# Hybrid decoder step on one core: key pass with eight page slots, weight pairs on ScalarE's queue, paired transposes and narrower stationary queries

## The chip, the cores and the metric

The kernel runs on one core of a Trainium2 chip. The metric is the device time of one execution in microseconds (us). TensorE is called PE below, its weight loads PEld, VectorE DVE, ScalarE ACT, GpSimd POOL, SyncE SP.

## The reference

One inference step of a two-layer decoder. The prompt has 512 tokens, and beside it 8 sequences decode 4 new tokens each; the width is 2048. All data are float32.

1. Layer 0: `[b, c, h, z] = rmsnorm(x) W_in`, `y = (silu(z) * b * conv3(c * h)) W_out`, `x = x + y`.
2. Keys and values, shared by all later layers: `k, v = rmsnorm(x) W_kv`; k is normalised per head (16 half heads of 128) and its first 32 components are rotated.
3. Layer 1, differential attention: `q, z = rmsnorm(x) W_in_b`; q is normalised and rotated like k. Prompt queries attend causally to prompt keys; each of the 8 sequences attends to 2048 past keys, which lie in 16 pages of 128 keys in a paged cache (`cache_k`, `cache_v`, `page_table`), and to its 4 new keys. `w = softmax(s0) - lambda * softmax(s1)`, `o = w v`, `y = (rmsnorm(o) * silu(z)) W_out_b`.

What the changed code computes is the projections of point 2 and 3, and the past scores of the 8 sequences:

```python
k_past = cache_k[page_table].reshape(n_seq, past, N_HEADS, 2, HEAD_DIM)
s_past = jnp.einsum('bqhcd,bkhcd->bhcqk', q, k_past, preferred_element_type=jnp.float32)
```

## The kernel before

The program runs six stages one after the other: `read_inputs`, `conv_in`, `conv_out`, `project_and_score`, `attention`, `project_out`. Only `project_and_score` (line 677 on) changes.

**Projections.** The stage makes 64 blocks of 128 output columns, called steps n = 0 to 63: 16 of q, 16 of z, 16 of k, 16 of v. A weight block is split into a high and a low part, and PE multiplies x_hi and x_lo by w_hi (line 1032, 64 matmuls of 272 columns) and then x_hi by w_lo (line 1040, 32 matmuls). Weights come as pairs of blocks of 2 MB each (`load_pair`, line 778, issued on SP's queue) into two buffers. ACT scales a pair by the norm gain in 16 instructions (`scale_pair`, line 834), makes w_hi (`split_hi`, line 848), and DVE makes w_lo (`split_lo`, line 947). DVE takes the result of a block out of PSUM (`evacuate`, lines 956 and 958), and after a squared sum (PE line 1048) and ACT's rsqrt it finishes the tile (`finish`, lines 971 to 986). ACT stores the tile to a scratch in HBM (`store`, line 854) three steps later; tiles of k and v are also turned on PE (lines 1062, 1065), copied (lines 859, 860) and written out (lines 862, 864).

**Key pass.** Beside steps 18 to 63 the stage computes the past scores. The keys of one sequence and one half of the heads are 16 half pages of 512 KB; there are 256 of them. SP loads them (`load_keys`, line 790) into a ring of six slots. The work is cut into 128 units; four half pages make two units, an even and an odd one. DVE transposes a unit in blocks of 32x32 with four instructions (`turn_unit`, line 996) into one of two buffers; PE then multiplies it (`score`, line 1081): 16 float32 matmuls of 128 columns, which the profile shows as 32, since each is run as two. The stationary operand is 32 columns wide, of which 16 can be other than zero: 4 queries in each of 4 blocks of rows, laid in `q_blocks` by ACT (`lay_queries`, line 890). The four column groups of the array work side by side. A slot is free when both units of its pages have been transposed.

**Order.** Each engine's instructions are one list in program order. How many units a step gets is written in `UNITS_IN_STEP`. Unit A stands before `finish` on DVE and in the middle of the step on PE, C at the end, and D after it:

```python
for n in range(N):                      # DVE
    evacuate(n - 1)
    turn_unit(units["A"])
    finish(n - 2)
    split_lo(n + 1)
    for at in "BCD": turn_unit(units[at])
```

(shortened: units that a step lacks are left out.) On PE a step is: first half of line 1032, D of the step before, second half, A, squared sum of n - 1, first half of line 1040, B, `turn_tile(n - 2)`, second half, C. On ACT a step is: `square(n - 1)`, `split_hi(n + 1)`, `store(n - 3)`, `norm_scale(n - 1)`, in some steps `lay_queries` and `move_scores`, and in even steps `scale_pair(n // 2 + 1)`. SP's list has `load_pair(n // 2 + 1)` at the start of every even step and four `load_keys` for each odd unit. `finish` and, for v, `evacuate` write into one of two tiles, and wait until the store of the tile two steps earlier has landed (`scratch_out`).

Of the kernel before, what the change touches and what calls it, by code (L numbers as in the profile page):

```python
# [21 lines left out]
ALU = mybir.AluOpType  # L22
# [616 lines left out]
NRING = 6  # L639
# [7 lines left out]
UNITS_IN_STEP = [2, 2, 2, 3] * 4 + [3, 3, 3, 2] * 4 + [4, 3, 4, 3, 3, 4, 3] * 2  # L647
# [31 lines left out]
def project_and_score(nc, m, d, st):  # L679
# [10 lines left out]
    with ExitStack() as ctx:  # L690
# [8 lines left out]
        swap = sb("swap", [ROT, T])  # L699
        cos, sin = sb("cos", [ROT, T]), sb("sin", [ROT, T])  # L700
        rows = [sb(f"rows{s}", [P, TT * P]) for s in range(2)]
        srows = [sb(f"srows{s}", [GS, G * P]) for s in range(2)]
        pages = sb("page_ids", [1, NSEQ * NPG], I32)
        ring = [sb(f"ring{s}", [P, HALF]) for s in range(NRING)]
        kth = [sb(f"keys_turned{f}", [P, GRP * QUAD]) for f in range(2)]
        qblk = [sb(f"q_blocks{f}", [P, HALF]) for f in range(2)]
# [10 lines left out]
        rows_out = [sem(f"rows_out{s}") for s in range(2)]  # L717
        page_in = [sem(f"page_in{s}") for s in range(NRING)]
        blank, qblk_ready, kt_ready, unit_scored = sem("blank"), sem("qblk_ready"), sem("kt_ready"), sem("unit_scored")
# [27 lines left out]
        def rows_in_slot(n):  # L747
            return sum(turns(x) for x in range(n % 2, n, 2))

# [16 lines left out]
        def _(sp):  # L766
# [3 lines left out]
            def load_pair(p):  # L770
                w, col0, _ = head_weights(d, KINDS[2 * p // KT])
                col = col0 + (2 * p % KT) * P
                if p == 1:
                    sp.wait_ge(lo_ready, 1)
                else:
                    sp.wait_ge(block_done, 2 * p - 2)
                sp.sem_inc(granted, 1)
                sp.dma_start(tiles(m.PAIR_RAW[p % 2]),
                             w.rearrange("(k p) n -> p k n", p=P)[:, :, col:col + 2 * P]).then_inc(pair_in[p % 2], 16)

            def load_keys(n):
# [8 lines left out]
                sp.dma_start(ring[n % NRING][:, :], cache_k[ds(page, 1), :, hh * HALF:(hh + 1) * HALF]  # L790
# [29 lines left out]
        def _(act):  # L820
# [4 lines left out]
            scratch = {"q": d["q_scratch"], "k": d["k_scratch"], "z": d["z_scratch"]}  # L825

# [23 lines left out]
            def store(n):  # L850
# [5 lines left out]
                if turns(n):  # L856
                    act.wait_ge(turned, turns_before(n) + 1)
                    after(act, rows_out[s], rows_in_slot(n) * 32)
                    act.activation(rows[s][:, :], m.PS[:, ROWS, :], ACT.Copy).then_inc(rows_ready, 1)
                    act.activation(srows[s][:, :], m.PS[0:GS, SROWS, 0:G * P], ACT.Copy).then_inc(rows_ready, 1)  # L860
                    act.wait_ge(rows_ready, turns_before(n) * 2 + 2)
                    act.dma_start(out_p[kind][:, :, local * P:(local + 1) * P],
                                  rows[s][:, :].rearrange("p (t c) -> p t c", t=TT)).then_inc(rows_out[s], 16)
                    act.dma_start(out_s[kind][:, :, local * P:(local + 1) * P],
                                  srows[s][:, :].rearrange("p (g c) -> p g c", g=G)).then_inc(rows_out[s], 16)
# [17 lines left out]
            def lay_queries(half):  # L883
# [4 lines left out]
                for b in range(P // TURN):  # L888
                    for c in range(4):
                        ins = act.activation(  # L890
                            qblk[half % 2][b * TURN:(b + 1) * TURN, :].rearrange("p (m c x) -> p m c x", m=PART, c=4)
# [43 lines left out]
            for s in range(2):  # L935
                act.wait_ge(scratch_out[s], 16 * kept_in_slot(N + s))
                act.wait_ge(rows_out[s], 32 * rows_in_slot(N + s))
# [89 lines left out]
        def _(pe):  # L1027
# [40 lines left out]
            def score(u):  # L1068

                half, b = u // 8, u // 4  # L1070
                if u % 8 == 0:
                    pe.wait_ge(qblk_ready, half + 1)
# [738 lines left out]
```

## Time and profile before

| | |
|---|---|
| time, median of 3 runs | 2752.18 us (2747.29 to 2761.38) |
| the profiled execution: its time, its span | 2754.07 us, 2752.3 us |
| granted TensorE clock, mean | 0.956 of full speed |
| busy share of the span: PE, PEld, DVE, ACT, POOL | 90%, 81%, 54%, 37%, 13% |
| `project_and_score` | 1033.0 to 2073.2 us of the span |
| of it, steps 18 to 63 with the key pass | 1273.6 to 2057.3 us |

A line of the profile names the line of the kernel, the engine and the operation, what is written and what is read (out<-in, buffer numbers left out) and its shape. In a timeline a row gives the start and the length in us, xcount if several equal instructions are merged, and in square brackets the idle time of that engine just before, with what ended it. A DMA's row is only its issue; how long it took to land is told in a line of its own.

### The profile page before, as it was taken

To read this page: it belongs to the slowest core of one execution; us is meant where nothing else is said; L and a number is where in the kernel's file an instruction comes from. 1 tells how busy PE (TensorE), PEld (TensorE's weight loads), DVE (VectorE), ACT (ScalarE), POOL (GpSimd) and SP (SyncE) were. 2 spreads that over 40 slices of the span, in tenths; PEclk is the share of its full clock that TensorE was granted. 3 is DMA by queue.
4 is the path that set the end of the run, shared out by engine and by line. 5 is a ranking of instruction groups with operands and counts; after the bars stand their busy time and mean duration, and the time that the engine had idled before them with its cause. 6 is when DMAs were issued, how large, how long until landed. Compare 5 with 4: busy or idle time off the path is not lost. (4 is left out here: it accounts for less than half of the span.)

```text
span 2752.3 us, 52718 instructions
## 1 busy us (share of the span) xinstructions
PE 2481.1 (90%) x21599; PEld 2229.3 (81%) x21599; DVE 1494.2 (54%) x1926; ACT 1017.1 (37%) x1826; POOL 346.9 (13%) x142
## 2 busy tenths in 40 slices
PE   6999999999999999999999999989995556656998
PEld 5999999999999989999898999978882122213998
DVE  3565565666563343456888887766664334324221
ACT  4121111112112226776445687745541212224121
POOL 5233333233320110000000000000000110010000
PEclk9999999999999999999999999999997778877999
DMA  4323332323323323244766778778869989986343
GB/s 129 92 77 92 92 92 76 92 83 85 92 76 112 112 86 99 85 153 135 248 237 239 268 266 267 266 243 267 281 231 361 385 343 374 381 363 245 113 120 87
DMA packets 387584, 512.01 MB, mean 186 GB/s; under 512 B 12618, under 2 KB 319700, under 8 KB 370964
## 3 DMA queue, kind: packets, MB, share of 16 engines
q1 hardware_dynamic: 328436, 449.67, 48.1%
q10 hardware_dynamic: 57792, 55.74, 5.8%
q0 software_dynamic: 1200, 4.46, 0.4%
q8 instruction: 106, 1.74, 0.3%
q14 instruction: 50, 0.41, 0.0%
HBM read 470.87 MB, written 38.94 MB: 185 GB/s over the span
## 5 line engine op out<-in xcount | busy, mean ns | idle before, releaser
L1032 PE MATMUL psum<-x_hi,w_hi 128*128 128x272 f32 x2048 | 434.2, 293 | 3.0 <-PEq L503 3.0
L106 PE MATMUL psum<-x_hi,w_hi 128*128 128x272 f32 x2048 | 427.0, 289 | 8.4 <-DVEq L413 8.4
L106 PE MATMUL psum<-x_lo,w_hi 128*128 128x272 f32 x2048 | 426.2, 289 | 0.0
L1032 PE MATMUL psum<-x_lo,w_hi 128*128 128x272 f32 x2048 | 426.0, 289 | 0.0
L996 DVE STREAM_TRANSPOSE h_keys_turned<-h_ring 128x512 f32<-128x512 f32 x512 | 325.1, 682 | 144.3 <-DMA h_ring<-in_cache_k_dram 140.6
L1032 PEld LDWEIGHTS psum<-x_hi,w_hi 128*128 128x128 f32 x2048 | 321.7, 190 | 18.8 <-issue 18.8
L106 PEld LDWEIGHTS psum<-x_hi,w_hi 128*128 128x128 f32 x2048 | 321.5, 189 | 9.5 <-ACTq L405 9.1
L1032 PEld LDWEIGHTS psum<-x_lo,w_hi 128*128 128x128 f32 x2048 | 322.4, 189 | 0.0
L106 PEld LDWEIGHTS psum<-x_lo,w_hi 128*128 128x128 f32 x2048 | 320.9, 188 | 0.0
L366 POOL TENSOR_TENSOR w_raw<-w_raw,params 128x2048 f32<-128x2048 f32 x63 | 245.9, 3903 | 509.6 <-DMA w_raw<-in_w_in_a_dram 502.7
L1040 PE MATMUL psum<-x_hi,w_lo 128*128 128x272 f32 x2048 | 287.1, 296 | 0.0
L1040 PEld LDWEIGHTS psum<-x_hi,w_lo 128*128 128x128 f32 x2048 | 267.0, 190 | 9.4 <-issue 5.9
L114 PE MATMUL psum<-x_hi,w_lo 128*128 128x272 f32 x2048 | 266.4, 287 | 0.0
L114 PEld LDWEIGHTS psum<-x_hi,w_lo 128*128 128x128 f32 x2048 | 260.2, 188 | 0.0
L834 ACT ACTIVATE w_raw<-w_raw,params 128x256 f32<-128x256 f32 x496 | 201.6, 495 | 103.9 <-DMA w_raw<-in_w_kv_dram 58.6
L385 ACT ACTIVATE w_hi<-w_raw 128x2048 fp32r<-128x2048 f32 x64 | 122.4, 1912 | 305.1 <-PE psum L114 280.4
L422 DVE TENSOR_TENSOR w_lo<-w_raw,w_hi 128x2048 fp32r<-128x2048 f32 x64 | 175.5, 2742 | 104.1 <-ACT w_hi L385 104.1
L947 DVE TENSOR_TENSOR w_lo<-w_raw,w_hi 128x2048 fp32r<-128x2048 f32 x63 | 143.6, 2280 | 54.6 <-ACT w_hi L848 54.6
L1081 PE MATMUL psum<-h_keys_turned,h_q_blocks 128*32 128x128 f32 x4096 | 141.2, 280 | 35.1 <-DVE h_keys_turned L996 34.9
L1489 PE MATMUL psum<-head 128*128 128x128 f32 (+3 forms) x128 | 49.3, 518 | 126.4 <-DMA head<-out_new_v_prompt_dram 125.7
L1533 PE MATMUL psum<-ring,weights 128*8 128x512 f32 x1024 | 146.0, 671 | 8.0 <-DMA ring<-in_cache_v_dram 8.0
L1081 PEld LDWEIGHTS psum<-h_keys_turned,h_q_blocks 128*32 128x32 f32 x4096 | 106.4, 111 | 55.8 <-DVE h_keys_turned L996 29.3
(207 smaller groups left out, 3134.7 us busy)
## 6 DMA issues: line engine op xcount, KB each, us to landing
h_ring<-in_cache_k_dram SPq DMA_DIRECT2D x256, 512.0 KB, 6.1
ring<-in_cache_v_dram SPq DMA_DIRECT2D x128, 1024.0 KB, 12.5
w_raw<-in_w_in_a_dram SPq DMA_DIRECT2D x64, 1024.0 KB, 6.2
w_raw<-in_w_kv_dram SPq DMA_DIRECT2D x16, 2048.0 KB, 12.7
w_raw<-in_w_in_b_dram SPq DMA_DIRECT2D x15, 2048.0 KB, 9.6
w_raw<-in_w_out_a_dram SPq DMA_DIRECT2D x16, 1024.0 KB, 5.6
f_raw<-in_w_out_b_dram SPq DMA_DIRECT2D x16, 1024.0 KB, 6.1
x_scratch<-x ACTq DMA_DIRECT2D x16, 272.0 KB, 2.0
```

The source lines that it names most:

```text
L106: pe.matmul(out[:, g, 0:GT], m.WH[s][:, k * P:(k + 1) * P], x[:, k * T + g * GT:k * T + (g + 1) * GT], start=(k == 0 and x is xh), stop=Fa ...
L114: last = pe.matmul(out[:, g, 0:GT], m.WL[s][:, k * P:(k + 1) * P], xh[:, k * T + g * GT:k * T + (g + 1) * GT], start=False, stop=(k == KT ...
L366: pool.tensor_tensor(tiles(raw[p % 2][:, :]), tiles(raw[p % 2][:, :]), m.PAR[:, GA:GA + KT].unsqueeze(2).to_broadcast([P, KT, P]), ALU.mul ...
L385: act.activation(m.WH[p % 2][:, :], raw[p % 2][:, :], ACT.Copy).then_inc(hi_ready, 1)
L422: dve.tensor_tensor(m.WL[p % 2][:, :], raw[p % 2][:, :], m.WH[p % 2][:, :].bitcast(F32), ALU.subtract).then_inc(lo_ready, 1)
L834: ins = act.activation(wk, wk, ACT.Copy, scale=m.PAR[:, gain + k:gain + k + 1])
L947: dve.tensor_tensor(columns(m.PAIR_LO, n), src, tiles(m.WH[n % 2][:, :].bitcast(F32)), ALU.subtract).then_inc(lo_ready, 1)
L996: dve.transpose(kth[u % 2][:, s * QUAD:(s + 1) * QUAD], ring[n % NRING][:, u % 2 * QUAD:(u % 2 + 1) * QUAD]).then_inc(kt_ready, 1)
L1032: pe.matmul(psum[n % 2][:, g, 0:GT], m.WH[n % 2][:, k * P:(k + 1) * P], x[:, k * T + g * GT:k * T + (g + 1) * GT], start=(k == 0 and x is ...
L1040: last = pe.matmul(psum[n % 2][:, g, 0:GT], w[:, k, :], m.XH[:, k * T + g * GT:k * T + (g + 1) * GT], start=False, stop=(k == KT - 1), ski ...
L1081: last = pe.matmul(bank[a * TURN:(a + 1) * TURN, u // 2 % 2, :, u % 2, :], qblk[half % 2][:, ch * TURN:(ch + 1) * TURN], keys[:, :, a * 4 ...
L1533: last = pe.matmul(out[c * B:c * B + 2 * NEW, :], wt[r % 2][:, weights_at(p, c):weights_at(p, c) + 2 * NEW], ring[(r * NPG + p) % NR][:, c ...
```

## The change

1. The ring of half pages has eight slots in place of six, as one buffer, and a `turn_unit` is two instructions of 128x1024 elements (two pages each) in place of four of 128x512.
2. `load_pair` moves from SP to ACT: at step 0 after `split_hi(1)`, and in even steps after `split_hi(n + 1)`, before `store(n - 3)`.
3. `q_blocks` has 16 columns per block in place of 32, so the score matmul has a stationary operand of 16 columns and writes 16 of each 32 rows of PSUM; DVE sets the two banks to zero once at the start.
4. `rows` and `srows`, the buffers from which k and v tiles are written out, become single; `swap` lies in `r`.
5. `UNITS_IN_STEP` is spread otherwise: 2 or 3 units in the steps of z, three in nearly all of v.

```diff
-NRING = 6
+NRING = 8
+QN = P // 32 * NEW
-UNITS_IN_STEP = [2, 2, 2, 3] * 4 + [3, 3, 3, 2] * 4 + [4, 3, 4, 3, 3, 4, 3] * 2
+UNITS_IN_STEP = [2, 3] * 8 + [3, 3, 3, 2] * 4 + [3, 3, 4, 3, 3, 3, 3] * 2
...
-        rows = [sb(f"rows{s}", [P, TT * P]) for s in range(2)]
-        srows = [sb(f"srows{s}", [GS, G * P]) for s in range(2)]
+        rows = sb("rows", [P, TT * P])
+        srows = sb("srows", [GS, G * P])
-        ring = [sb(f"ring{s}", [P, HALF]) for s in range(NRING)]
+        ring = sb("ring", [P, NRING * HALF])
-        qblk = [sb(f"q_blocks{f}", [P, HALF]) for f in range(2)]
+        qblk = [sb(f"q_blocks{f}", [P, HALF // TURN * QN]) for f in range(2)]
...
         def _(sp):
-            def load_pair(p):
-                w, col0, _ = head_weights(d, KINDS[2 * p // KT])
-                col = col0 + (2 * p % KT) * P
-                if p == 1:
-                    sp.wait_ge(lo_ready, 1)
-                else:
-                    sp.wait_ge(block_done, 2 * p - 2)
-                sp.sem_inc(granted, 1)
-                sp.dma_start(tiles(m.PAIR_RAW[p % 2]),
-                             w.rearrange("(k p) n -> p k n", p=P)[:, :, col:col + 2 * P]).then_inc(pair_in[p % 2], 16)
...
-                    sp.wait_ge(kt_ready, (2 * (before // GRP) + 1) * GRP + before % GRP + 1)
+                    sp.wait_ge(kt_ready, (2 * (before // GRP) + 1) * 2 + before % GRP // 2 + 1)
...
-            load_pair(1)
             sp.wait_ge(ids_in, 16)
             for n in range(N):
-                if n % 2 == 0 and n and n + 2 < N:
-                    load_pair(n // 2 + 1)
...
         def _(act):
+            def load_pair(p):
+
+                w, col0, _ = head_weights(d, KINDS[2 * p // KT])
+                col = col0 + (2 * p % KT) * P
+                if p == 1:
+                    act.wait_ge(lo_ready, 1)
+                else:
+                    act.wait_ge(block_done, 2 * p - 2)
+                act.dma_start(tiles(m.PAIR_RAW[p % 2]), w.rearrange("(k p) n -> p k n", p=P)[:, :, col:col + 2 * P]).then_inc(pair_in[p % 2], 16)
...
                 if turns(n):
                     act.wait_ge(turned, turns_before(n) + 1)
-                    after(act, rows_out[s], rows_in_slot(n) * 32)
+                    after(act, rows_out, turns_before(n) * 32)
...
             scale_second()
+            split_hi(1)
+            load_pair(1)
...
-                if n + 1 < N:
+                if n and n + 1 < N:
                     split_hi(n + 1)
+                if n and n % 2 == 0 and n + 2 < N:
+                    load_pair(n // 2 + 1)
                 if n >= 3:
                     store(n - 3)
...
             def turn_unit(u):
 
                 after(dve, unit_scored, u - 1)
-                for s in range(GRP):
-                    n = u // 2 * GRP + s
+                for pair in range(GRP // 2):
+                    n = u // 2 * GRP + 2 * pair
                     if u % 2 == 0:
-                        dve.wait_ge(page_in[n % NRING], 16 * (n // NRING + 1))
-                    dve.transpose(kth[u % 2][:, s * QUAD:(s + 1) * QUAD],
-                                  ring[n % NRING][:, u % 2 * QUAD:(u % 2 + 1) * QUAD]).then_inc(kt_ready, 1)
+                        for x in (n, n + 1):
+                            dve.wait_ge(page_in[x % NRING], 16 * (x // NRING + 1))
+                    dve.transpose(kth[u % 2][:, pair * 2 * QUAD:(pair + 1) * 2 * QUAD].rearrange("p (s x) -> p s x", s=2),
+                                  ring[:, n % NRING * HALF:(n % NRING + 2) * HALF].rearrange("p (s x) -> p s x", s=2)
+                                  [:, :, u % 2 * QUAD:(u % 2 + 1) * QUAD]).then_inc(kt_ready, 1)
...
+            dve.memset(m.PS[:, KEYS[0]:KEYS[0] + 2, :], 0.0).then_inc(blank_banks, 1)
...
-                pe.wait_ge(kt_ready, (u + 1) * GRP)
+                pe.wait_ge(kt_ready, (u + 1) * 2)
...
-                        last = pe.matmul(bank[a * TURN:(a + 1) * TURN, u // 2 % 2, :, u % 2, :],
-                                         qblk[half % 2][:, ch * TURN:(ch + 1) * TURN], keys[:, :, a * 4 + c, :],
+                        last = pe.matmul(bank[a * TURN:a * TURN + QN, u // 2 % 2, :, u % 2, :],
+                                         qblk[half % 2][:, ch * QN:(ch + 1) * QN], keys[:, :, a * 4 + c, :],
```

## Rows read from the trace of the kernel before

**Rows 1.** Windows: stretch, PE, PEld, DVE, ACT, POOL busy, PE clock, DMA share, GB/s.

```profile
1273.60:1495.30 221.70, 209.74 (x2339) 197.82 (x2337) 188.80 (x217) 107.99 (x253) 0.00 (x0) 0.98 0.67 230
1495.30:1765.10 269.80, 267.84 (x3060) 249.76 (x3056) 221.52 (x323) 200.70 (x406) 0.00 (x0) 1.00 0.79 264
1765.10:1784.40 19.30, 17.36 (x208) 16.04 (x203) 14.18 (x22) 11.88 (x24) 0.00 (x0) 1.00 0.88 311
1784.40:1808.90 24.50, 17.73 (x202) 16.25 (x198) 13.28 (x21) 15.19 (x39) 0.00 (x0) 0.93 0.41 134
1808.90:1828.50 19.60, 16.40 (x203) 15.23 (x199) 12.11 (x17) 5.67 (x16) 0.00 (x0) 1.00 0.95 333
1828.50:2057.30 228.80, 219.51 (x2706) 203.38 (x2702) 152.06 (x215) 114.86 (x299) 0.00 (x0) 0.99 0.80 267
```

**Rows 2.** Waits, 1273.6 to 2057.3: total us, times, longest.

```profile
DVE h_keys_turned L996 <- DMA h_ring<-in_cache_k_dram: 140.6, 85, 5.0
...
PE psum L1081 <- DVE h_keys_turned L996: 34.9, 23, 5.4
...
DVE h_tile L956 <- DMA k_scratch<-h_tile: 12.8, 2, 9.9
```

**Rows 3.** Timeline of PE and PEld around a score unit, and one step later.

```profile
1701.57 1.08 PE L1081 MATMUL psum<-h_keys_turned,h_q_blocks 128*32 128x128 f32 x32
1702.58 0.30 PEld L1032 LDWEIGHTS psum<-x_hi,w_hi 128*128 128x128 f32 x2 [0.20 <-issue]
...
1718.82 1.08 PE L1081 MATMUL psum<-h_keys_turned,h_q_blocks 128*32 128x128 f32 x32
```

**Rows 4.** Timeline of PE, cut 0.03 and 0.18 us into this unit.

```profile
1701.57 0.32 PE L1081 MATMUL psum<-h_keys_turned,h_q_blocks 128*32 128x128 f32 x4
...
1701.57 0.43 PE L1081 MATMUL psum<-h_keys_turned,h_q_blocks 128*32 128x128 f32 x8
```

**Rows 5.** Value matmuls of `attention`: timeline of PEld, and the stretch's window row.

```profile
2092.58 0.15 PEld L1533 LDWEIGHTS psum<-ring,weights 128*8 128x8 f32 x4 [0.70 <-issue]
...
2090.90:2095.20 4.30, 4.29 (x24) 0.73 (x24) 1.90 (x2) 0.00 (x0) 0.00 (x0) 0.50 1.01 419
```

**Rows 6.** Timeline of DVE, one unit transposed.

```profile
1352.41 2.47 DVE L996 STREAM_TRANSPOSE h_keys_turned<-h_ring 128x512 f32<-128x512 f32 x4
```

**Rows 7.** Landing of line 778 (pairs, from 1273.6), 790 (pages), 854 (scratch), in this order.

```profile
DMA to landing us min/median/max: 9.3/12.4/14.1
...
DMA to landing us min/median/max: 3.1/6.1/11.3
...
DMA to landing us min/median/max: 2.4/6.7/11.0
```

**Rows 8.** Timeline of steps 26 and 27 (z): a pair is scaled, split, and unit C follows.

```profile
1413.00 6.51 ACT L834 ACTIVATE w_raw<-w_raw,params 128x256 f32<-128x256 f32 x16 [6.84 <-DMA w_raw<-in_w_in_b_dram]
...
1419.96 1.90 ACT L848 ACTIVATE w_hi<-w_raw 128x2048 fp32r<-128x2048 f32 x1
...
1423.81 2.29 DVE L947 TENSOR_TENSOR w_lo<-w_raw,w_hi 128x2048 fp32r<-128x2048 f32 x1
...
1428.54 1.08 PE L1081 MATMUL psum<-h_keys_turned,h_q_blocks 128*32 128x128 f32 x32 [0.45 <-DVE h_keys_turned L996]
```

**Rows 9.** Timeline of step 49, the second of v.

```profile
1791.52 0.53 ACTq L854 DMA_DIRECT2D k_scratch<-h_tile  x1
...
1796.09 0.72 DVE L956 TENSOR_TENSOR h_tile<-psum,rs 128x544 f32<-128x544 f32 x1 [9.88 <-DMA k_scratch<-h_tile]
...
1799.26 1.94 PE L1081 MATMUL psum<-h_keys_turned,h_q_blocks 128*32 128x128 f32 x32 [5.36 <-DVE h_keys_turned L996]
```

**Rows 10.** Timeline of the stage's end: the last two tiles written out.

```profile
2066.64 0.38 ACTq L862 DMA_DIRECT2D out_new_v_prompt_dram<-h_rows  x1
...
2068.30 0.60 ACT L859 ACTIVATE h_rows<-psum 128x512 f32<-128x512 f32 x1 [1.69 <-PE psum L1065]
```

**Rows 11.** Timeline of the stage's start.

```profile
1034.86 4.79 ACT L841 ACTIVATE w_raw<-w_raw,params 128x128 f32<-128x128 f32 x16 [2.14 <-POOL h_q_blocks L817]
```

More of the change, by code:

```diff
@@ L716, in project_and_score @@
         scratch_out = [sem(f"scratch_out{s}") for s in range(2)]
-        rows_out = [sem(f"rows_out{s}") for s in range(2)]
+        rows_out = sem("rows_out")
         page_in = [sem(f"page_in{s}") for s in range(NRING)]
+        blank_banks = sem("blank_banks")
         blank, qblk_ready, kt_ready, unit_scored = sem("blank"), sem("qblk_ready"), sem("kt_ready"), sem("unit_scored")
@@ L745, in kept_in_slot @@
             return sum(kind_of(x) != "v" for x in range(n % 2, n, 2))
-        def rows_in_slot(n):
-            return sum(turns(x) for x in range(n % 2, n, 2))
         def after(eng, sem_, n):
@@ L786, in load_keys @@
                     before = n - NRING
-                    sp.wait_ge(kt_ready, (2 * (before // GRP) + 1) * GRP + before % GRP + 1)
+                    sp.wait_ge(kt_ready, (2 * (before // GRP) + 1) * 2 + before % GRP // 2 + 1)
                 page = sp.value_load(pages[0:1, i * NPG + p:i * NPG + p + 1], min_val=0, max_val=n_phys - 1)
                 sp.sem_inc(granted, 1)
-                sp.dma_start(ring[n % NRING][:, :], cache_k[ds(page, 1), :, hh * HALF:(hh + 1) * HALF]
+                sp.dma_start(ring[:, n % NRING * HALF:(n % NRING + 1) * HALF], cache_k[ds(page, 1), :, hh * HALF:(hh + 1) * HALF]
                              .rearrange("o p n -> (o p) n")).then_inc(page_in[n % NRING], 16)
@@ L857, in store @@
                     act.wait_ge(turned, turns_before(n) + 1)
-                    after(act, rows_out[s], rows_in_slot(n) * 32)
-                    act.activation(rows[s][:, :], m.PS[:, ROWS, :], ACT.Copy).then_inc(rows_ready, 1)
-                    act.activation(srows[s][:, :], m.PS[0:GS, SROWS, 0:G * P], ACT.Copy).then_inc(rows_ready, 1)
+                    after(act, rows_out, turns_before(n) * 32)
+                    act.activation(rows[:, :], m.PS[:, ROWS, :], ACT.Copy).then_inc(rows_ready, 1)
+                    act.activation(srows[:, :], m.PS[0:GS, SROWS, 0:G * P], ACT.Copy).then_inc(rows_ready, 1)
                     act.wait_ge(rows_ready, turns_before(n) * 2 + 2)
                     act.dma_start(out_p[kind][:, :, local * P:(local + 1) * P],
-                                  rows[s][:, :].rearrange("p (t c) -> p t c", t=TT)).then_inc(rows_out[s], 16)
+                                  rows[:, :].rearrange("p (t c) -> p t c", t=TT)).then_inc(rows_out, 16)
                     act.dma_start(out_s[kind][:, :, local * P:(local + 1) * P],
-                                  srows[s][:, :].rearrange("p (g c) -> p g c", g=G)).then_inc(rows_out[s], 16)
+                                  srows[:, :].rearrange("p (g c) -> p g c", g=G)).then_inc(rows_out, 16)
             def square(n):
@@ L890, in lay_queries @@
                         ins = act.activation(
-                            qblk[half % 2][b * TURN:(b + 1) * TURN, :].rearrange("p (m c x) -> p m c x", m=PART, c=4)
+                            qblk[half % 2][b * TURN:(b + 1) * TURN, :].rearrange("p (m c x) -> p m c x", m=PART, c=4, x=QN)
                             [:, :, c, b * NEW:(b + 1) * NEW],
@@ L936, in _ @@
                 act.wait_ge(scratch_out[s], 16 * kept_in_slot(N + s))
-                act.wait_ge(rows_out[s], 32 * rows_in_slot(N + s))
+            act.wait_ge(rows_out, 32 * turns_before(N))
             act.wait_ge(half_out, 16 * HALVES)
@@ L964, in finish @@
                     return
-                t, t32 = tile[s], tile[s][0:ROT, :]
+                t, t32, swap = tile[s], tile[s][0:ROT, :], r[s][0:ROT, :]
                 keep = {"q": st.QS, "k": st.KS, "z": st.ZS}[kind]
@@ L981, in finish @@
                     dve.sem_inc(granted, 1)
-                    chain.link(dve.stream_shuffle(swap[:, :], t32, [(i + half) % ROT for i in range(ROT)]))
-                    chain.link(dve.tensor_tensor(swap[:, :], swap[:, :], sin[:, :], ALU.mult))
+                    chain.link(dve.stream_shuffle(swap, t32, [(i + half) % ROT for i in range(ROT)]))
+                    chain.link(dve.tensor_tensor(swap, swap, sin[:, :], ALU.mult))
                     chain.link(dve.tensor_tensor(t32, t32, cos[:, :], ALU.mult))
-                    chain.link(dve.tensor_tensor(t32, t32, swap[:, :], ALU.add))
+                    chain.link(dve.tensor_tensor(t32, t32, swap, ALU.add))
                 dve.tensor_copy(keep[:, local * G * GS:(local + 1) * G * GS].rearrange("p (g t) -> p g t", g=G),
@@ L1070, in score @@
                 half, b = u // 8, u // 4
+                if u == 0:
+                    pe.wait_ge(blank_banks, 1)
                 if u % 8 == 0:
```

1 line of the change is left out of this document (removed).

## The prediction

> **What bounds the kernel now.** The page's shares come first: PE is busy for 90% of the span. Then the windows of the changed stage, steps 18 to 63, by kind of step: z, k, the three steps 48, 49 and 50 around the change from k to v, and the rest of v [rows 1]. Stretch less PE busy gives the idle time: 12.0 + 2.0 + 1.9 + 6.8 + 3.2 + 9.3 = 35.1 us. Beside it the clock column: (1 - clock) x stretch is 4.4, 1.7 and 2.3 us in z, step 49 and v, 8.4 in all; part of it lies in the idle time itself, so I take 6. So of 783.7 us PE loses 41, and the rest is its own work: 46 steps of 96 projection matmuls with 128 units between them. Next the waits [rows 2]: all of PE's idle time is put down to turned keys, and DVE, which turns them, waited 140.6 us for half pages, in 85 waits of at most 5.0, and 12.8 us for two stores of k tiles. PE is the bound, and only what makes keys late can be won. A clean step shows it: from score to score one step on is 17.25 us without a gap [rows 3].
>
> **Eight slots.** With six, turning the odd unit of group j frees the slots into which half of group j+1 is loaded, and the next unit needs these at once; a page lands 6.1 us after its issue, up to 11.3 [rows 7]. With eight, group j+1 is already under way and the freed slots take j+2, needed three units, some 16 us, later. Four pages are 2 MB, 5.0 us at the 419 GB/s of [rows 5]; even behind a pair that is under 16. So the 140.6 us of page waits nearly go. What they cost PE is at most 35.1 less the share of the two stores (6.8 in step 49, and 1.4 in step 50, where its one other gap is a page): 27 us.
>
> **Two pages per transpose.** Four instructions take 2.47 us, 0.60 from start to start [rows 6]; so one is 0.67 long. Against the 2.29 us for 2048 elements [rows 8] that is 1.05 ns per element, 0.54 for 512, and 0.06 per start. No row has 1024. Bounds: nothing saved, and two starts per unit, 0.12 us, 15 us of DVE's time in all; a loss I exclude, since both pages stay runs of 512 elements. DVE is 85% busy in z and 66% in v [rows 1], so on PE's path I count nothing; it is cover.
>
> **Sixteen columns.** The stationary operand shrinks, the 128 moving columns do not. The first four matmuls end 0.32 us after the start, eight end at 0.43 [rows 4]: a beat of 0.11 us per four, eight beats per unit. Does the weight load or the stream set the beat? The value matmuls have 8 stationary columns: four per 0.85 us, 512 columns, at clock 0.50, that is 1.2 GHz [rows 5]. By 4 for the columns and 2 for the clock that is 0.106 us, the same beat with a quarter of the weights. So the stream sets it, and only the unit's first load is exposed: between 0 and 0.03 us x 128. I take 1.7 us. The Trainium skill, "TensorE: Matmul & The Clock Gate", section "LDWEIGHTS (loading the stationary operand)", has the load's time go with its columns over 1.2 GHz: 13 ns less for each of 32 loads, by which 55 us would be won if loads lay on the path; the beat of the 8-column matmuls says that they don't. The memset of the banks (0.9 us on an idle DVE) is hidden before the first split. `q_blocks` is half as large, so the two memsets that ACT waits for [rows 11] end about 0.9 us sooner, and with them the first pair's issue, for which PE idles in step 1: 0.9 us won.
>
> **Pairs on ACT's queue.** This is the part that can hurt. Three things stand behind a pair now. (a) *Its own landing.* In the key stage it was 9.3 us at the least, 12.4 in the median [rows 7], in one queue with the pages: only pages issued before it delayed it. In a queue of its own it shares the DMA engines with pages issued after it too: one group of four adds 5 us, so L, from issue to landing, is 10 to 17 us, by where the odd units fall. The Trainium skill, "DMA: Bandwidth & Descriptors", section "Queues, rings and completion order", says that each DMA engine takes the queues in turn, a packet at a time; by that rule pairs would be later still than by my bounds, and no row here shows two queues sharing. What needs L? In z: after landing, scale 6.5, exp 0.5, w_hi 1.9, w_lo 2.3 [rows 8], then unit C 2.5, since C stands behind `split_lo` in DVE's list; with 0.3 for the issue that is L + 14.0. PE wants C in the odd step. A bare step is (209.7 - 31 x 1.2)/14 = 12.3 us (31 units of 1.08 plus switching [rows 1, 3]); the even step with two units is 14.7, and C is wanted 8.2 + 1.2 + 4.1 = 13.5 into the next: 28.2. So L may be 14. The last row of [rows 8] is this chain, 0.45 late, when two waits for pages came on top. The new spread puts three units into just these odd steps. In three of seven z pairs the group freed at the even step's start comes beside the pair, L about 16: 2 us each, 6 us. In k the squared sum comes first: L + 7.5 against 17.2 + 10.6, so 20; in v 18. There I count 1 us and 2.5 us, the latter with what pages still cost at a DMA share over 0.80. (b) *Scratch stores of even steps* are issued behind the pair and land with it, about 18 us after the step's start; `finish` needs them at 19 to 20 (before: 6.7 us, at most 11.0 [rows 7]). Covered, by 1 to 2 us; without that cover 1 us per pair. (c) *The last k tile.* `evacuate(49)` waits, in step 50, for a store that is now issued right behind pair 26. Pair 12.4, store 1, evacuation 0.7, unit A 2.4, from 1 us before the step's start: 15.5; PE wants A at 8.2. Idle 7.2 and 1 us of half clock: 8.2, where 3.2 are lost now [rows 1]. DVE, stopped there, also holds up C, the next evacuation and the pages. Step 49 has the same wait without a pair: now 9.88 us on DVE and 5.36 on PE [rows 9], because ACT, late with `move_scores` and the scaling, issued the store only 7 us into the step. The new spread moves `move_scores` from 48 to 49: issue at 5, landing 4.5, evacuation and A 3.1, wanted at 9.4: 3.2 left. The issue's own wait, for block n - 1, is one that `split_hi(n + 1)` has just passed, so it adds none; the issue itself takes some 0.5 us of ACT's sequencer, as the scratch store's [rows 9], 22 times, while ACT works on the 1.9 us of w_hi: nothing. SP loses a wait and gains nothing else.
>
> **Single rows buffers.** Within the stage a step lies between uses, the landing 6 us: nothing. At the end the last copy must wait until the stores of the tile before have landed. They are issued at 2066.6 and right behind it, at 2067.0 [rows 10], and the quickest store took 2.4 us [rows 7]: 2069.4 in place of 2068.3, 1.1 us lost, on the path.
>
> **Spread.** Unit counts are the same, so PE's work is; v drops to 44 units from 48, z gets 35 for 31. Counted above.
>
> **Sum.** Losses after: z 6, k 1, step 48 0.5, step 49 3.2, step 50 8.2, v 2.5: 21.4, for 41 now; 19.6 won. Start 0.9, columns 1.7 won, end 1.1 lost: 21.1 us. From the profiled execution's 2754.1 (span 2752.3 and 1.8 around it) that is 2733.0; that execution lies 1.9 above the median, so 2731 us.
>
> **Rivals.** What a measurement can tell from no change is 0.5%, 13.8 us: below 2738.4 or above 2765.9.
> - *Pairs become the bound (slower).* Place: ACT's wait at the scaling. Price: in z 7 us for each us of L over 14, in v 7 over 18. Without my 6 for z the losses are 15.4; they reach 41 at L = 17.6, and slower by 13.8 begins near 19. At L = 20: 42 + 14 + 15.4 = 71, time 2781. For it: pages run nearly always, 0.67 to 0.80 of the engines [rows 1]. Against: two whole groups would have to come beside every pair (9.3 + 10). 7%.
> - *Half of it comes back (same).* L near 16 in all seven z pairs (14 us), stores in (b) late by 1 us for 15 pairs beyond their cover (5 us on PE): 13 us less won, 2744. For it: ACT has no slack in odd steps of z; against: in half of them no group is freed near the issue. 24%.
> - *Nothing stays idle.* L under 14 throughout, step 50 as short as 49: 16 us more, 2715. It needs pairs as quick as now. 10%.
> - *The weight load sets the beat.* Then half the columns halve it at most, 8 x 0.055 us x 128 = 56 us, 2676. For it: the load of 32 columns recurs with every matmul; against it, [rows 5]. By the skill's rule above it would be the same 55. 2%.
>
> **How the numbers follow.** The forecast, 2731, has 57%, its own range 2720 to 2741 (one us of L in z, 2 to 5 us of step 50, the bounds of the columns). Outside 2714 to 2753 lie the first and the last rival and a little of the second and third. Faster: nine tenths of the forecast's 57, 10, 2 and 3 of the second rival, 66%; same 27%; slower 7%.
>
> **What would show it.** DVE's wait for pages from 140.6 to under 30 us. Pages land in 5 to 8 us in the median, pairs in 13 to 16. The score beat stays 0.11 us per four. The step after the k-to-v change has PE's longest gap, 5 to 9 us before a unit A, ended by DVE behind a `k_scratch` landing; z shows gaps of 1 to 3 us before C in odd steps. I am wrong if pairs land after 18 us, if gaps in k appear before line 1048, or if page waits stay.

## The result and the profile after

The changed kernel takes 2790.26 us (median of 4 runs, 2786.20 to 2801.12) where the kernel before takes 2754.41 (4 runs on the same chip, 2747.29 to 2761.38): a ratio of 1.0136, 95% interval 1.0096 to 1.0177. I had forecast 2731, faster. It is slower by 36 us, outside my range. The profiled execution took 2801.12 us, its span 2799.3 us at a mean granted clock of 0.947; its steps 18 to 63 last from 1279.3 to 2103.3 us, 824.0 us for 783.7 before.

Windows of the changed kernel, the six stretches of [rows 1] in the same order and with the same columns (here and below the line numbers shift a little from kernel to kernel):

```profile
1279.30:1507.05 227.75, 216.85 (x2434) 204.00 (x2433) 192.82 (x162) 108.34 (x252) 0.00 (x0) 0.96 0.69 235
1507.05:1792.03 284.98, 272.22 (x3093) 252.08 (x3089) 215.86 (x237) 206.55 (x423) 0.00 (x0) 0.99 0.76 254
1792.03:1809.78 17.75, 17.47 (x207) 15.96 (x203) 15.67 (x18) 8.92 (x23) 0.00 (x0) 1.00 0.98 338
1809.78:1835.60 25.82, 18.53 (x199) 16.80 (x199) 11.24 (x13) 17.32 (x38) 0.00 (x0) 0.87 0.40 146
1835.60:1862.03 26.43, 17.53 (x170) 16.40 (x167) 11.03 (x10) 12.31 (x36) 0.00 (x0) 0.81 0.65 214
1862.03:2103.30 241.27, 220.95 (x2614) 204.50 (x2614) 136.21 (x116) 104.28 (x264) 0.00 (x0) 0.95 0.67 236
```

Stretch less PE busy is 60.4 us of idle time, for 35.1 before, and the clock fell in z, in steps 49 and 50 and in v. The waits in steps 18 to 62, 1279.3 to 2087.9 (what waited, for what; total, times, longest):

```profile
DVE w_lo L945 <- ACT w_hi L842: 82.2, 17, 14.4
...
ACT w_raw L828 <- DMA w_raw<-in_w_kv_dram: 42.4, 8, 24.1
PE psum L1084 <- DVE h_keys_turned L995: 42.4, 13, 8.9
...
DVE h_tile L954 <- DMA k_scratch<-h_tile: 30.1, 2, 15.1
...
DVE h_keys_turned L995 <- DMA h_ring<-in_cache_k_dram: 12.7, 5, 5.2
...
DVE h_r L969 <- DMA z_scratch<-h_tile: 8.7, 5, 3.5
```

The wait that the slots were to remove is gone: DVE waited 12.7 us for pages where it waited 140.6 [rows 2]. PE still names turned keys, for 42.4 us in 13 waits, but DVE is now late for another reason: it makes w_lo before units C and D, and w_lo waits for w_hi, that for the scaling, and that for the pair. The pairs' landing and the store's issue show it (line 819 is the pair, line 848 the scratch store; the first row is issue to landing at least, median, most; in the others the three numbers are the length of the issue itself in ns):

```profile
DMA to landing us min/median/max: 8.7/16.9/27.1
...
L848 ACTq DMA_DIRECT2D z_scratch<-h_tile x16: 520/3681/11128, 1295.8 to 1542.5; - x16
L848 ACTq DMA_DIRECT2D k_scratch<-h_tile x16: 526/1244/11323, 1562.7 to 1834.6; - x16
```

Before, pairs took 12.4 us in the median and 14.1 at most [rows 7]. And an issue that is 0.53 us long where it stands alone [rows 9] now takes up to 11.3 us behind a pair, with ACT's sequencer held the whole time (this is called the hold below). Timeline of ACT in steps 58 and 59 (v), and of PE at the end of this chain:

```profile
1990.54 0.40 ACTq L819 DMA_DIRECT2D w_raw<-in_w_kv_dram  x1
...
2003.14 3.81 ACT L884 ACTIVATE h_q_blocks<-q_sample 32x32 f32<-32x32 f32 x16 [9.97 <-issue]
2013.97 6.50 ACT L828 ACTIVATE w_raw<-w_raw,params 128x256 f32<-128x256 f32 x16 [7.02 <-DMA w_raw<-in_w_kv_dram]
2020.56 1.91 ACT L842 ACTIVATE w_hi<-w_raw 128x2048 fp32r<-128x2048 f32 x1
2022.50 2.29 DVE L945 TENSOR_TENSOR w_lo<-w_raw,w_hi 128x2048 fp32r<-128x2048 f32 x1 [14.17 <-ACT w_hi L842]
...
2027.13 1.91 PE L1084 MATMUL psum<-h_keys_turned,h_q_blocks 128*16 128x128 f32 x32 [8.59 <-DVE h_keys_turned L995]
```

Two suspects stand in it: ACT held 9.97 us by an issue, and then, the hold over, still 7.02 us of waiting for the pair, which landed 23.4 us after its issue. The timeline of the stage's start shows a third loss, which I had not expected: SP issues the eight pages at once, ahead of the first pair.

```profile
1036.96 8.19 SPq L777 DMA_DIRECT2D h_ring<-in_cache_k_dram  x8
...
1043.46 0.42 ACTq L819 DMA_DIRECT2D w_raw<-in_w_in_b_dram  x1
1058.80 6.48 ACT L828 ACTIVATE w_raw<-w_raw,params 128x256 f32<-128x256 f32 x16 [17.76 <-DMA w_raw<-in_w_in_b_dram]
```

Step 1 is 24.7 us from its first matmul to the next step's, for 19.8 before.

### The profile page after: what moved, and what is told of

It is laid out like the page before. It is cut to its first block and busy times, and to the rows that moved or that the text cites. A ratio compares the mean times of both kernels' runs of the same rounds, so it can differ in the third digit from the quotient of the medians.

```text
span 2799.3 us, 52498 instructions
## 1 busy us (share of the span) xinstructions
PE 2494.4 (89%) x21599; PEld 2240.6 (80%) x21599; DVE 1479.2 (53%) x1671; ACT 1018.3 (36%) x1826; POOL 346.9 (12%) x142
## 3 DMA queue, kind: packets, MB, share of 16 engines
q10 hardware_dynamic: 121776, 120.75, 12.7%
## 5 line engine op out<-in xcount | busy, mean ns | idle before, releaser
L995 DVE STREAM_TRANSPOSE h_keys_turned<-h_ring 128x1024 f32<-128x1024 f32 x256 | 300.4, 1216 | 33.5 <-PE psum L1084 20.6
L1041 PE MATMUL psum<-x_hi,w_lo 128*128 128x272 f32 x2048 | 293.0, 299 | 0.0
L1041 PEld LDWEIGHTS psum<-x_hi,w_lo 128*128 128x128 f32 x2048 | 272.9, 194 | 10.3 <-issue 6.1
L114 PE MATMUL psum<-x_hi,w_lo 128*128 128x272 f32 x2048 | 266.4, 287 | 0.0
L114 PEld LDWEIGHTS psum<-x_hi,w_lo 128*128 128x128 f32 x2048 | 260.1, 188 | 0.0
L1084 PE MATMUL psum<-h_keys_turned,h_q_blocks 128*16 128x128 f32 x4096 | 139.7, 278 | 42.4 <-DVE h_keys_turned L995 42.4
L1084 PEld LDWEIGHTS psum<-h_keys_turned,h_q_blocks 128*16 128x16 f32 x4096 | 102.5, 97 | 63.1 <-DVE h_keys_turned L995 30.7
## 6 DMA issues: line engine op xcount, KB each, us to landing
ring<-in_cache_v_dram SPq DMA_DIRECT2D x128, 1024.0 KB, 12.6
```

Of the source, the lines that this page charges most:

```text
L114: last = pe.matmul(out[:, g, 0:GT], m.WL[s][:, k * P:(k + 1) * P], xh[:, k * T + g * GT:k * T + (g + 1) * GT], start=False, stop=(k == KT ...
L995: dve.transpose(kth[u % 2][:, pair * 2 * QUAD:(pair + 1) * 2 * QUAD].rearrange("p (s x) -> p s x", s=2), ring[:, n % NRING * HALF:(n % NRI ...
L1041: last = pe.matmul(psum[n % 2][:, g, 0:GT], w[:, k, :], m.XH[:, k * T + g * GT:k * T + (g + 1) * GT], start=False, stop=(k == KT - 1), ski ...
L1084: last = pe.matmul(bank[a * TURN:a * TURN + QN, u // 2 % 2, :, u % 2, :], qblk[half % 2][:, ch * QN:(ch + 1) * QN], keys[:, :, a * 4 + c, ...
```

## The experiments

Unless said otherwise an edit is made to the changed kernel. Each ratio is to the kernel before, timed beside it. There were three series, on three chips, in which the kernel before took 2753.0 us (experiments 1 to 4), 2759.4 us (5, 6, 10 and 11) and 2754.8 us (7, 8, 9 and 12); runs of different series are to be compared by their ratios.

**1. Undo the pairs' move.** `load_pair` is back in SP's list; slots, transposes, columns, spread and single buffers stay. (The edit is shown shortened; the pair of step 0 moves too.)

```diff
-                    load_pair(n // 2 + 1)      # in ACT's list, after split_hi(n + 1)
+                    load_pair(n // 2 + 1)      # in SP's list, at the start of even steps
```

> The changed kernel with its weight pairs on SP's queue again, all else kept. Theory 1 (pairs on ACT's queue cost all of the loss, by holding ACT's sequencer at the next store, by landing late, and by lying behind the first eight pages): the time falls to the forecast, 2725 to 2740 us; no store's issue on ACT lasts over 3 us; pairs land in 10 to 14 us; step 1 is as before. Rival (the slots, the paired transposes, the single rows buffers or the spread cost it): it stays above 2760 us.

Measured: 2722.03 us, ratio 0.9883 (0.9866 to 0.9899), a little below the range that I expected. Pairs land after 9.5, 12.4 and 14.8 us (least, median, most), no store's issue lasts over 2.5 us, and step 1 is 19.3 us long. The other parts together win 31 us, and the move turns this into a loss of 36. Its windows are nearly the bare work, with the clock full everywhere but in step 49:

```profile
1271.60:1483.10 211.50, 209.60 (x2434) 197.13 (x2432) 191.20 (x161) 107.91 (x252) 0.00 (x0) 1.00 0.72 251
1483.10:1754.10 271.00, 268.88 (x3093) 249.78 (x3089) 216.89 (x238) 205.87 (x423) 0.00 (x0) 1.00 0.78 269
1754.10:1771.30 17.20, 17.20 (x206) 15.94 (x202) 15.59 (x18) 10.79 (x24) 0.00 (x0) 1.00 0.99 327
1771.30:1794.20 22.90, 18.77 (x202) 17.07 (x198) 11.23 (x13) 14.98 (x36) 0.00 (x0) 0.85 0.46 180
1794.20:1809.40 15.20, 15.20 (x172) 14.40 (x167) 10.83 (x10) 5.28 (x20) 0.00 (x0) 1.00 1.04 344
1809.40:2022.70 213.30, 213.30 (x2614) 198.18 (x2614) 138.03 (x117) 111.57 (x280) 0.00 (x0) 1.00 0.78 269
```

**2. The move alone** (part 2 of the change), made to the kernel before.

> The kernel before with part 2 alone: pairs on ACT's queue, six slots, old spread. Theory 1: slower than the changed kernel, 2795 to 2830 us, since it keeps the page waits (35 us) and adds the loss of the queue (about 60 us less what both share). Rival: near the kernel before, 2745 to 2765 us, and the loss lies in the other parts.

Measured: 2796.99 us, ratio 1.0165 (1.0145 to 1.0185): +44 us. The pairs of `w_kv` landed after 12.5, 14.9 and 18.3 us (least, median, most), the longest store issue was 8.8 us. With six slots DVE's waits for pages stay (128.3 us in 80 waits), and PE waits 51.8 us for turned keys where it waited 34.9; how much of this is late landing and how much the hold, this run can't tell.

**3. The store ahead of the pair,** so that it isn't held.

```diff
-                if n and n % 2 == 0 and n + 2 < N:
-                    load_pair(n // 2 + 1)
                 if n >= 3:
                     store(n - 3)
+                if n and n % 2 == 0 and n + 2 < N:
+                    load_pair(n // 2 + 1)
```

> The changed kernel with load_pair moved behind store(n - 3) on ACT, so that no store is issued right behind a pair of the same step. Theory 1a (what costs is ACT's sequencer, held at the store's issue behind the pair): most of the loss goes, 2740 to 2760 us, stores issue in 0.5 us, the gap in step 50 before unit A falls from 8.9 to about 3 us; the 5 us of step 1 stay. Theory 1b (what costs is the pair's own late landing, which this doesn't mend): above 2780 us.

Measured: 2820.04 us, ratio 1.0241 (1.0224 to 1.0259). The scratch stores were no longer held (three stores of scores still took 3.6 to 7.2 us) and the time grew by 30 us; the theory that the hold is the loss fell in this form. Line 848 as above, then the waits from 1273 to 2105:

```profile
L848 ACTq DMA_DIRECT2D z_scratch<-h_tile x16: 520/527/545, 1297.6 to 1541.5; - x16
L848 ACTq DMA_DIRECT2D k_scratch<-h_tile x16: 527/532/718, 1568.9 to 1861.7; - x16
```
```profile
DVE w_lo L945 <- ACT w_hi L842: 154.4, 21, 15.0
ACT w_raw L828 <- DMA w_raw<-in_w_kv_dram: 153.7, 16, 23.3
ACT w_raw L828 <- DMA w_raw<-in_w_in_b_dram: 63.4, 6, 16.0
```

Pairs need as long as in the changed kernel (`w_kv` 16.9 us in the median), and from step 36 on they are issued 3 to 7 us later, since `store` waits for the turned tile first. A late issue adds to a late landing.

**4. The first pages wait for their step,** as they did behind the pairs' waits.

```diff
                 if n == FIRST_UNIT_STEP - 4:
+                    sp.wait_ge(block_done, n)
```

> The changed kernel, with SP made to wait for block 14 before it issues the first eight pages, as the pair loads on its list made it wait before. Theory: the first pair lands in 8 to 9 us in place of 15.3, step 1 is 19 us long in place of 24.7, and the whole is 5 us shorter, about 2785 us. Rival: step 1 is long because of the issue on ACT; then nothing changes.

Measured: 2791.65 us (2781.14 to 2795.12), ratio 1.0123 (1.0099 to 1.0146), not distinguishable from the changed kernel. Step 1 fell to 17.8 us, but the same thing happened 190 us later, where the eight pages now meet pair 8:

```profile
1221.98 0.38 ACTq L820 DMA_DIRECT2D w_raw<-in_w_in_b_dram  x1
1222.15 8.31 SPq L777 DMA_DIRECT2D h_ring<-in_cache_k_dram  x8
1241.47 6.49 ACT L829 ACTIVATE w_raw<-w_raw,params 128x256 f32<-128x256 f32 x16 [8.69 <-DMA w_raw<-in_w_in_b_dram]
```

That pair landed after 19.5 us, step 15 grew from 13.0 to 21.8, and the 6.9 us won at the start were gone. With the pairs on SP's queue the same burst is harmless (in experiment 1 this pair lands after 10.4 us and step 15 is 13.0 us long): pages issued behind a pair in its own queue wait behind it.

**5 and 6. Who issues, and what is held.** In 5 GpSimd issues the pairs; in 6 the pairs stay on ACT's queue and GpSimd issues all stores of tiles and rows, so that nothing of theirs stands behind a pair. (Both edits are shown shortened.)

```diff
         def _(pool):                       # 5
+            load_pair(1)
+            for n in range(2, N - 2, 2):
+                load_pair(n // 2 + 1)
...
         def _(pool):                       # 6; ACT's store(n) keeps the two copies of rows
+            for n in range(N):
+                store(n)
```

> The changed kernel with the weight pairs on GpSimd's queue, which has nothing else to do in this stage: the pairs still have a queue apart from the pages, but nothing of ScalarE's stands behind them. Theory H (the loss is the store's issue that holds ScalarE's sequencer behind the pair): the issues of the stores fall back to some 0.5 us each and the time to 2722-2730, as with the pairs on SP's queue. Theory L (a pair on a queue apart from the pages gets its share packet for packet and lands late, whoever issues it): the pairs of w_kv still land at a median of 16-18 us after their issue, and the time is 2745-2765, with w_lo's waits on the scaled pair still at some 60 us. Theory L is the one I lean to for half of the loss, so some 2750.

> The changed kernel with the pairs left on ScalarE's queue, and the stores (scratch, rows, sample rows) issued by GpSimd instead of ScalarE, so that only a pair and once in four steps the scores stand in ScalarE's queue. Theory H (hold): 2722-2735, no issue of ScalarE over 0.6 us. Theory L (late landing): the pairs of w_kv land at a median near 17 us still, and the time is 2750-2770. If both count, this and the run with the pairs on GpSimd's queue come out alike.

Measured: 5 takes 2730.37 us, ratio 0.9894 (0.9878 to 0.9911); 6 takes 2787.41 us, ratio 1.0108 (1.0089 to 1.0127). So they did not come out alike. In 6 no store of a tile or of rows holds ACT (two stores of scores took 4.2 and 4.8 us), and little or nothing is won: the ratios of 6 and of the changed kernel (1.0136, 1.0096 to 1.0177) overlap; the landing of all pairs, who waited for it, and ACT's waits:

```profile
  ACT w_raw L843: 192.4, 21
...
DMA to landing us min/median/max: 8.8/18.4/24.4
```
```profile
ACT w_raw L843 <- DMA w_raw<-in_w_kv_dram: 124.3, 15, 19.4
ACT w_raw L843 <- DMA w_raw<-in_w_in_b_dram: 68.0, 6, 15.5
```

In the changed kernel these two waits are 42.4 and 32.1 us. Its hold was therefore in large part time in which ACT would have waited for the same pair a few instructions later: taken away, it came back there as 118 us of waiting. It is no clean test of the hold, though, since the pairs also landed later (18.4 us in the median for 16.9). What makes the pair late is its queue. But in 5 the pairs have a queue of their own too, and those of `w_kv` land after 13.2, 14.5 and 18.6 us. At the stage's end 5 is 13 us behind experiment 1: some 6 us are lost at the start, where step 1 is 24.3 us long, and 7 in z (218.7 us for 211.5), but next to none in k and v. The queues' rows from 1273 to 2050, first of 6, then of 5 (packets, MB, share of the engines), tell the two apart:

```profile
q1 hardware_dynamic: 34560, 125.84, 46.0%
q10 hardware_dynamic: 47424, 49.81, 19.1%
```
```profile
q1 hardware_dynamic: 35712, 130.04, 48.4%
q0 software_dynamic: 11616, 46.14, 16.4%
```

q1 carries the pages, in packets of 3.6 KB on average. On ACT's queue, q10, a packet is 1.05 KB on average (49.81 MB by 47,424); on GpSimd's, q0, it is 3.97 KB. The Trainium skill, "DMA: Bandwidth & Descriptors", section "SWDGE vs HWDGE vs iDMA", has packets on GpSimd's path hold preferably at most 4096 B; the row agrees. Whether the length of the packets is what helps is tested in 7.

**7. Pages in packets of 1 KB.** If queues take turns by packets, shorter packets of pages must give the pair its share back. Each page is loaded by four transfers of 256 columns (`QW`), and DVE waits for all four (edit shortened).

```diff
-                sp.dma_start(ring[:, n % NRING * HALF:(n % NRING + 1) * HALF], cache_k[ds(page, 1), :, hh * HALF:(hh + 1) * HALF]
+                for x in range(4):
+                    sp.dma_start(ring[:, n % NRING * HALF + x * QW:n % NRING * HALF + (x + 1) * QW],
+                                 cache_k[ds(page, 1), :, hh * HALF + x * QW:hh * HALF + (x + 1) * QW]
```

> The changed kernel with each page of 512 KB loaded by four transfers of 256 columns, so that the packets of a page are as long as those of a pair (1 KB a row of a partition) where they were 4 KB. Pairs stay on ScalarE's queue. Theory P (two queues take turns packet for packet, so that the short packets of the pair get the small share): the pair now gets about half of the bytes, and lands at a median of 10-14 us in k and v where it landed at 17; the pages land later (8-11 us where 6.5), and the time falls by 15-40 us from 2790 unless the pages become late. Rival D (the pair is late because the 16 DMA engines are full, whatever the packets): it lands at 17 us or later, and the time is 2790 or more.

Measured: 2778.38 us, ratio 1.0094 (1.0077 to 1.0110). The pairs of `w_kv` landed after 11.9, 12.7 and 14.7 us. The queues while both have work and a pair is in flight, 1658 to 1662 in the changed kernel, then 1643 to 1649 here:

```profile
q1 hardware_dynamic: 346, 1.28, 78.8%
q10 hardware_dynamic: 351, 0.36, 25.3%
```
```profile
q10 hardware_dynamic: 1142, 1.14, 55.4%
q1 hardware_dynamic: 1007, 0.92, 47.5%
```

In both the two queues move nearly equal numbers of packets. So with long packets beside it the pair gets 90 GB/s (0.36 MB in 4 us), and with equal ones 190 GB/s (1.14 MB in 6 us). The landing theory holds. The time fell by only 12 us where I had expected 15 to 40, since the price went to the pages:

```profile
DVE h_keys_turned L998 <- DMA h_ring<-in_cache_k_dram: 154.5, 50, 10.3
```

**8. Six slots** in the version of experiment 1 (`NRING = 6`).

> The version with the pairs on SP's queue, with six page slots where it has eight; two pages per transpose, 16-column queries and the new spread stay. It sizes the slots. If the slots carry the gain (VectorE's 140 us of waits for pages come back and with them the 35 us of TensorE's idle time), it is 2745-2755; if the halved number of transposes carries it, 2722-2728. A pair of pages comes free at once now, so that six slots are three pairs, which speaks for the first: I expect 2745.

Measured: 2792.83 us, ratio 1.0146 (1.0129 to 1.0163): 71 us more than with eight, and slower than the kernel before, which has six slots as well. DVE's waits for pages, 1273 to 2105:

```profile
DVE h_keys_turned L996 <- DMA h_ring<-in_cache_k_dram: 198.0, 52, 5.9
```

52 waits of 3.8 us on average, for 85 of 1.7 before: two pages are waited for and freed at a time. I had expected 2745. So two pages per transpose cost much without the two more slots. That it is they and not the new spread or the single buffers is argued from these waits; experiment 10 shows the spread to be harmless with eight slots only. Eight slots with one page per transpose were not run, so whether the slots alone would win the 31 us stays open.

**9. Sixteen columns alone,** in the kernel before.

> The kernel before with the 16-column queries alone (and what they need: the two score banks are blanked once). The beat of the score matmuls is set by the 256-column stream and not by the weight load, so this is worth the 1.7 us that I gave it (the smaller memset and cheaper laying of queries), inside the noise: ratio 0.998-1.002. Rival (the weight load sets the beat): 2690 or less.

Measured: 2752.32 us (10 runs), ratio 0.9993 (0.9982 to 1.0003). The mean score matmul is 277 ns long, 280 before.

**10 to 12. The spread, and a better version.** 10 is experiment 1 with the old `UNITS_IN_STEP`. 11 is experiment 1 with the scratch stores of k blocks 46 and 47 issued a step earlier, ahead of `scale_pair`. 12 is both. (The edit is shown shortened; `store` leaves these two out.)

```diff
+                if n - 2 in (46, 47):
+                    keep(n - 2)            # the scratch store alone
                 if n % 2 == 0 and n + 2 < N:
                     scale_pair(n // 2 + 1)
```

> The version with the pairs on SP's queue, with the old spread of the units over the steps (2, 2, 2, 3 in z; 4, 3, 4, 3, 3, 4, 3 in v). It sizes the spread: if eight slots and paired transposes carry the 31 us that the other parts win, it stays within 3 us of 2722; if the spread carries half of them, it is 2735-2740. I expect 2724.

> The version with the pairs on SP's queue, with the scratch stores of the last two key blocks (46 and 47) issued before the scaling of the pair in steps 48 and 49 and not behind the split in steps 49 and 50. In step 49 the first v block's evacuation waits for store 46 to land, and TensorE's 4.1 us of idle stand behind it. If the store's place is what is late, the idle of step 49 goes and the time is 2717-2719; if the scaled pair is late anyway, it stays 2722.

> The best version that the runs point to: pairs on SP's queue, eight slots, paired transposes, 16-column queries, the old spread of the units, and the scratch stores of blocks 46 and 47 issued ahead of the scaling. The old spread was worth 2.5 us and left 6 us of idle time in step 49, and the early stores took that step's idle away: 2713, against 2715.4 and 2719.8 for each alone. Rival (the two do not add, since the old spread puts four units into step 50 or 52): 2716.

Measured: 10 takes 2719.84 us, ratio 0.9859 (0.9842 to 0.9875); 11 takes 2715.41, ratio 0.9842 (0.9825 to 0.9858); 12 takes 2716.49, ratio 0.9864 (0.9848 to 0.9880). The new spread wins nothing. 11 has the lowest time, 44 us below the kernel before in its series (7 runs); from 12 it can't be told, as the intervals overlap. Steps 49 and 50 of 11:

```profile
1770.50:1786.80 16.30, 16.30 (x202) 15.18 (x198) 11.32 (x13) 13.82 (x36) 0.00 (x0) 1.00 0.62 240
1786.80:1803.20 16.40, 15.18 (x170) 14.39 (x166) 9.98 (x9) 7.33 (x22) 0.00 (x0) 1.00 1.01 326
```

Step 49 has no idle time left, for 4.1 us in experiment 1; step 50 has 1.2 us. In 12 the old spread has `move_scores` in step 48 and step 49 keeps 3.9 us: the two edits don't add, as that run's rival said, though for another reason.

## Why the prediction was wrong, by its steps

The bare work can now be read: experiment 1 less its idle time, with step 49 from experiment 11, is 209.6 + 268.9 + 17.2 + 16.3 + 15.2 + 213.3 = 740.5 us. The kernel before lost 43.2 us against it, where I had 41. So the reading of what there was to win was right. What the changed kernel loses against it:

| stretch | z | k | step 48 | step 49 | step 50 | rest of v | sum |
|---|---|---|---|---|---|---|---|
| predicted | 6 | 1 | 0.5 | 3.2 | 8.2 | 2.5 | 21.4 |
| measured | 18.2 | 16.1 | 0.6 | 9.5 | 11.2 | 28.0 | 83.5 |

With the start (0.9 us won by forecast, 5.7 lost) this carries the whole miss: 62.1 + 6.6 is 68.7 us, for 68.1 between the 2733.0 forecast for the profiled execution and its 2801.1. That execution was the longest of the four; against the medians the miss is 59. Step by step of the prediction:

- **"Eight slots": right.** Waits for pages went from 140.6 to 12.7 us, below the 30 that I had named. The 31 us are what eight slots and paired transposes win together (experiment 1); paired transposes without the slots lose (experiment 8).
- **"Two pages per transpose": mis-sized.** DVE's 256 transposes took 300.4 us for 325.1, 24.7 us less where my upper bound was 15; it stayed off PE's path. That a pair of pages is freed and awaited at once, which costs much in a ring of six, I had not costed.
- **"Sixteen columns": right.** Experiment 9 has no measurable difference; the busy time of the score matmuls fell by 2.4 us, for the 1.7 I took.
- **"Pairs on ACT's queue", (a) its own landing: the step that failed.** I put L at 10 to 17 us and counted 2 us each for three of seven pairs in z. In z the seven pairs took 8.7, 18.2, 14.9, 16.8, 17.7, 17.6 and 13.4 us; the five pairs issued in steps 52 to 60 took 16.2, 22.5, 27.1, 23.4 and 19.6. The thresholds of z and v stood up: the excess over 14 in z is 15.2 us, for 18.2 lost, that over 18 in v 20.6, for 28.0. Experiment 5, without the hold, bears out the first: 12.6 us of excess in z, 9.1 lost. A part of each loss is the clock, which fell behind the gaps (PE busy is 20.6 us more than in experiment 1 for the same work). I had sized L as if pages delayed a pair by their bytes alone, at equal shares. In fact turns are by packets: a pair of 1 KB packets beside pages of 4 KB packets gets the small share as long as any page is in flight (experiment 7). I had the Trainium skill's rule of turns by packets in the text ("DMA: Bandwidth & Descriptors", section "Queues, rings and completion order"; the trace agrees, with 346 packets beside 351), and said that by it pairs would be later; I gave it no price and no chance of its own. The price was to be had from the length of the rows that a transfer copies, 1 KB for a pair and 4 KB for a page: a fifth of the 419 GB/s of [rows 5] is 84, by which 2 MB take 25 us, an estimate. At the 90 GB/s measured it is 23 us.
- **The issue, "some 0.5 us of ACT's sequencer ... nothing": wrong, the second step that failed.** It was the issue behind the pair's, not the pair's own, that was held, up to 11.3 us, and 146.9 us over the 48 scratch stores, for 25.4 before; stores of rows were held up to 10.9 us on top. What this costs stays open for the whole: experiment 6 is 8 us faster by the two ratios (1.0136 and 1.0108), less than their uncertainty, and its pairs landed later. In k, where I counted 1 us, 16.1 were lost though no L passed my threshold of 20, and there the hold is the likely cause. In step 40 the pair took 18.8 us and had landed 5 us before ACT came to scale it; step 41 took 23.8 us for 17.2, with this gap before the squared sum:

```profile
1674.52 6.50 ACT L828 ACTIVATE w_raw<-w_raw,params 128x256 f32<-128x256 f32 x16 [0.43 <-ACT h_scores_half L897]
1681.61 2.18 PE L1049 MATMUL psum<-h_r,ones 128*128 128x272 f32 x4 [3.80 <-ACT h_r L868]
```

  In experiment 5, without the hold, the pair of step 40 took 18.6 us and step 41 its bare 17.2, though there the pair was issued 2.5 us earlier in the step.
- **(b) stores "covered": nearly.** DVE waited 8.7 us in 5 waits for the landing of z tiles; whether any of it reached PE is not shown.
- **(c) the last k tile: mechanism and place right.** Step 50 has PE's longest gap of the key pass, 8.9 us before a unit A, ended by DVE behind a `k_scratch` landing; A began 17.2 us into the step where I had 15.5. With the half clock it is 11.2 for 8.2. Step 49's 9.5 for 3.2 is (a) only in part. With the pairs on SP's queue the store is issued 6.4 us into the step and not 5, and with the half clock step 49 loses 6.6 us: so much the term was too small by itself. The other 2.9 us are the late pair 25, which took 18.9 us; behind it ACT issued the store 10.7 us into the step.
- **"SP loses a wait and gains nothing else": wrong.** That wait had kept the first pages behind the first pair. Without it 5 us are lost at the start; with a wait for its step alone put back, the loss is 8.8 us at step 15 (experiment 4).
- **"Single rows buffers": right.** The last copy waited for a store to land, 0.9 us for the 1.1 I took.
- **"Spread": no gain.** Experiment 10 has the old spread and is not slower.
- **The signs.** Pairs that land after 18 us and a gap in k before the squared sum were the signs of being wrong that I had named, and both came.
- **The rivals.** "Pairs become the bound (slower)" came true, at its place and about at its price: I had 2781 for L = 20, and gave it 7%. I argued against it that two whole groups of pages would have to come beside every pair. That held only for shares by bytes.

## What to carry to other kernels

Before a transfer moves to a queue of its own, look at the packet size of what runs beside it: in one queue order protects an urgent transfer from what is issued later, in two it competes, and short packets lose. A rule that speaks against the change needs a price and a chance, not a mention. And when a hold or a wait is removed, ask what the engine would wait for next: with the stores off ACT's queue, 118 us of its time moved to the wait for the same pair, and the kernel was hardly faster.

## What the runs showed of the hardware

- SP's and ACT's queues, both with work on the same 16 DMA engines, moved 1007 and 1142 packets in 6 us when both had packets of at most 1 KB, and 346 (3.7 KB) and 351 (1.03 KB) in 4 us when one had longer ones.
- A transfer issued right behind one of 2 MB on ACT's queue held ACT's sequencer for up to 11.3 us, for 0.52 us alone. A timeline shows it as a long issue, and the instruction behind it as idle "issue":

```profile
1650.62 0.44 ACTq L819 DMA_DIRECT2D w_raw<-in_w_kv_dram  x1
...
1651.10 11.32 ACTq L848 DMA_DIRECT2D k_scratch<-h_tile  x1
...
1662.53 0.60 ACT L853 ACTIVATE h_rows<-psum 128x512 f32<-128x512 f32 x1 [9.53 <-issue]
```

- The queue that carried the pairs had packets of 1.05 KB on average when ACT issued them and of 3.97 KB when GpSimd did, for an issue of 1.15 us in place of 0.39.
